# Long convolution by table transforms: even frequencies folded a second time, tables stored in two parts

## The reference

```python
def _hyena(hy, spec, skip):
    L = hy.shape[1]
    u = hy.astype(jnp.float32)
    z, g1, g2 = u[..., :D_HYENA], u[..., D_HYENA:2 * D_HYENA], u[..., 2 * D_HYENA:]
    for o, gate in enumerate((g1, g2)):
        conv = jnp.fft.irfft(jnp.fft.rfft(z, n=2 * L, axis=1) * spec[:, o], n=2 * L, axis=1)[:, :L]
        z = gate * (conv + z * skip[o].astype(jnp.float32))
    return z
```

## Time and profile before

| what | value |
|---|---|
| median of 3 runs | 3564.7 us (3564.47 to 3573.62) |
| the profiled execution, its own time | 3566.57 us |
| its span in the profile | 3564.8 us |
| mean granted TensorE clock | 0.971 of 2.4 GHz |
| PE busy | 3332.7 us, 93% of the span |
| `phase_convolve`, PE's first to last matmul | 433.46 to 721.8 us |

### The profile page before, as it was taken

How to read it: one execution, slowest core, us unless ns; L and a number is a source line. 1 busy time by engine, 2 the same in 40 slices (tenths; PEclk the granted TensorE clock), 3 DMA queues, 4 the chain that set the end, 5 groups by cost and what they waited for, 6 DMA issues and landing times. The chain is left out here.

```text
span 3564.8 us, 40485 instructions
## 1 busy us (share of the span) xinstructions
PE 3332.7 (93%) x15544; PEld 2663.5 (75%) x15544; DVE 1758.4 (49%) x2739; ACT 1112.2 (31%) x2015; POOL 560.6 (16%) x378
## 2 busy tenths in 40 slices
PE   7999899976898899999999998988999899999998
PEld 5777688865786678888888776775567688888886
DVE  4415655565422446555544539789654332332434
ACT  4323344354322222111111433136674221211112
POOL 0002466722000001000001200000263200010010
PEclk9999999987999999999999999999999999999999
DMA  3232324412121113333321301123333121111111
GB/s 115 87 104 70 130 88 136 142 61 92 54 71 59 42 59 95 100 102 105 104 83 62 105 18 42 48 57 90 76 73 113 30 71 48 47 47 47 51 43 59
DMA packets 223644, 269.80 MB, mean 76 GB/s; under 512 B 17277, under 2 KB 150294, under 8 KB 221062
## 3 DMA queue, kind: packets, MB, share of 16 engines
q1 hardware_dynamic: 223496, 267.78, 24.4%
HBM read 219.16 MB, written 29.18 MB: 70 GB/s over the span
## 5 line engine op out<-in xcount | busy, mean ns | idle before, releaser
L193 PE MATMUL psum<-rounded,rounded 128*128 128x512 f32 (+2 forms) x3936 | 1537.7, 391 | 64.6 <-DVE rounded L222 51.6
L194 PE MATMUL psum<-rounded,rounded 128*128 128x512 f32 (+2 forms) x3936 | 1528.7, 388 | 0.0
L195 PE MATMUL psum<-rounded,rounded 128*128 128x512 f32 (+2 forms) x3936 | 1528.2, 388 | 0.0
L193 PEld LDWEIGHTS psum<-rounded,rounded 128*128 128x128 f32 x3936 | 746.6, 190 | 239.1 <-DVE rounded L222 56.8
L195 PEld LDWEIGHTS psum<-rounded,rounded 128*128 128x128 f32 x3936 | 746.1, 190 | 151.8
L194 PEld LDWEIGHTS psum<-rounded,rounded 128*128 128x128 f32 x3936 | 747.2, 190 | 148.9 <-issue 0.2
L3002 DVE TENSOR_TENSOR plain<-psum,plain 128x512 f32<-128x512 f32 x432 | 288.6, 688 | 110.4 <-PE psum L195 108.8
L3013 DVE TENSOR_TENSOR plain<-psum,plain 128x512 f32<-128x512 f32 x44 | 30.4, 692 | 425.1 <-ACT plain L2917 425.1
L3579 POOL TENSOR_TENSOR plain<-plain,plain 128x128 f32<-128x128 f32 (+3 forms) x64 | 97.3, 1530 | 563.4 <-ACT plain L3680 506.4
L3376 DVE TENSOR_SCALAR_CACHE_REDUCE plain<-plain,plain 128x384 bf16<-128x384 f32 (+2 forms) x204 | 181.8, 942 | 1.4
L2994 DVE TENSOR_TENSOR rounded<-plain,rounded 128x512 fp32r<-128x512 f32 x108 | 96.9, 897 | 166.0 <-ACT rounded L2906 165.9
(11 more groups left out here) (326 smaller groups left out, 3457.5 us busy)
## 6 DMA issues: line engine op xcount, KB each, us to landing
plain<-in_ff_w_dram SPq DMA_DIRECT2D x64, 512.0 KB, 5.4
plain<-in_w_ada_dram SPq DMA_DIRECT2D x96, 256.0 KB, 3.5
plain<-in_w_gu_dram SPq DMA_DIRECT2D x44, 512.0 KB, 5.0
plain<-in_w_in_dram SPq DMA_DIRECT2D x36, 512.0 KB, 4.0
rounded<-rounded SPq DMA_DIRECT2D x72, 256.0 KB, 3.4
plain<-in_c_fwd_dram SPq DMA_DIRECT2D x64, 256.0 KB, 2.6
plain<-in_w_down_dram SPq DMA_DIRECT2D x22, 512.0 KB, 3.7
fold<-plain SPq DMA_DIRECT2D x8, 1024.0 KB, 4.8
```

The lines of the kernel that those rows point to most:

```text
L193: nc.tensor.matmul(out, wh, xh, start=first, stop=False)
L194: nc.tensor.matmul(out, wh, xl, start=False, stop=False)
L195: return nc.tensor.matmul(out, wl, xh, start=False, stop=last)
```

## The change

A table is now stored in DRAM as two parts, high and rest, so a unit is 512 KB; ACT copies both with rounding in one instruction of 1024 columns, and POOL no longer takes part. Rows are put in another order: even rows, odd rows and their mirror images (`TOKENS`, `COLUMNS`), so that sums and differences of quarters can be formed. With them the signal's and the inverse's even frequencies need transforms over 256 rows instead of 512, and the odd ones share sums. The single rows that fall out of the symmetry (lags 0, 256, 512, 768) are stored by small DMAs and mended on one partition.

```diff
-FOLD_KB, HY_KB, HR_KB, HS_KB, ZFOLD_KB, DFT_RING_KB, MATS_KB, NYQ_KB = 6, 70, 118, 134, 150, 182, 198, 200.75
+FOLD_KB, HY_KB, HR_KB, HS_KB, ZFOLD_KB, DFT_RING_KB, MATS_KB, NYQ_KB, QUARTER_KB = 6, 70, 118, 134, 150, 182, 198, 201.5, 203.5
+SIGNAL_ORDER = (0, 1, 2, 3, 4, 6, 5, 7)
+SIGNAL_AT, INVERSE_AT, ROUND_UNITS = 16, 28, 36
...
-        self.core.nc.scalar.activation(self.ring[u % 4].hi, self.ring[u % 4].raw, ACT.Copy).then_inc(S["ft_hi"].sem, 1)
-
-    def low(self, pool, u):
...
+        self.core.nc.scalar.activation(self.ring[u % 4], self.raws[u % 4], ACT.Copy).then_inc(self.core.sig["ft_hi"].sem, 1)
...
+    for n, j in enumerate(SIGNAL_ORDER):
+        one, two = ps[:, (2 * n) % 8, :], ps[:, (2 * n + 1) % 8, :]
+        if n < 4:
+            pe.wait_ge(R.sem("act_free"), R.at("act_free", n + 5))
+        else:
+            pe.wait_ge(R.sem("dve_done"), R.at("dve_done", 2 * (n - 3)))
+        if j < 4:
+            cos, sin = ((0, 1), (6, 7)) if j < 2 else ((2, 3), (4, 5))
+            tables.products(pe, one, B + n, zfold, cos, True, j >= 2)
...
+            ins = tables.products(pe, two, B + n, zfold, sin, True, j != 0, block=2)
...
+        else:
+            u = B + 2 * n - 4
+            tables.products(pe, one, u, zfold, range(4, 8), True, True).then_inc(done, 1)
+            tables.products(pe, two, u + 1, zfold, range(0, 4), True, False)
+            mm3(nc, two, eighth[0:1, 0, :], eighth[0:1, 1, :], quarter.hi[0:1, 0, :], quarter.lo[0:1, 0, :], False, True).then_inc(done, 1)
...
+            tables.products(pe, one, B + n, y, (src, src + 1), True, False)
+            ins = tables.products(pe, two, B + n, y, (src + 2, src + 3), True, False, block=2)
...
+    pe.wait_ge(R.sem("y_lo"), R.at("y_lo", 8))
...
                 for n in range(4):
                     if R.o == 0:
                         load_folds(core, sp, folds[1], raws[1], 1, (n,))
                     else:
                         load_kept(core, sp, kept, n)
-                    tables.load_units(sp, B + 2 * UNITS + 4 + 2 * n, units[0:B + 2 * UNITS + 6 + 2 * n])
+                    tables.load_units(sp, at, units[0:at + 1])
+                    at += 1
...
             def fold_high(R, n):
                 act.wait_ge(R.sem("fold%d" % n), R.at("fold%d" % n, 16))
+                if n >= 1:
+                    act.wait_ge(R.sem("fold_fixed"), R.at("fold_fixed", 1))
...
-                    if 1 <= j <= 4:
-                        for n in (2 * j - 2, 2 * j - 1):
-                            act.wait_ge(R.sem("v_hi"), R.at("v_hi", n + 1))
-                            nc.scalar.activation(zfold.hi[:, n, :], zfold.raw[:, n, :], ACT.Copy).then_inc(R.sem("z_hi"), 1)
+                    if 1 <= j <= 2:
+                        act.wait_ge(R.sem("v_hi"), R.at("v_hi", j))
+                        nc.scalar.activation(zfold.hi[:, 4 * j - 4:4 * j, :], zfold.raw[:, 4 * j - 4:4 * j, :], ACT.Copy).then_inc(R.sem("z_hi"), 1)
...
+                for b in range(2):
+                    until(B + (signal_done(6) + 1, INVERSE_AT + 2)[b])
+                    for part, tiles in enumerate((slice(4 + b, TT, 2), slice(TT + b, TT + 4, 2))):
+                        act.wait_ge(R.sem("paired"), R.at("paired", 2 * b + part + 1))
+                        nc.scalar.activation(y.hi[:, tiles, :], y.raw[:, tiles, :], ACT.Copy).then_inc(R.sem("w_hi"), 1)
...
+                if R.o == 0:
+                    fold_low(rounds[1], 0)
+                    terms_of(R, 0)
+                    fix_folds(rounds[1])
+                    fold_low(rounds[1], 1)
+                    terms_of(R, 1)
+                    fold_low(rounds[1], 2)
+                    fold_low(rounds[1], 3)
+                    outputs(R, 0)
+                    outputs(R, 1)
+                    dve.wait_ge(R.sem("tile_gated"), R.at("tile_gated", 4))
+                else:
+                    terms_of(R, 0)
+                    outputs(R, 0)
+                    terms_of(R, 1)
+                    group_sums(0)
+                    group_sums(1)
+                    outputs(R, 1)
+                    group_sums(2)
+                    group_sums(3)
```

More of the change, by code:

```diff
@@ L73, in constants, with split_table @@
+def split_table(blocks):
+    x = np.stack(blocks)
+    short = lambda v: np.ldexp(np.round(np.ldexp(np.frexp(v)[0], 11)), np.frexp(v)[1] - 11)
+    high = short(x)
+    return np.concatenate([high, x - high], 2).astype(np.float32)
+def constants():
+    fwd, sig, inv, order = transforms()
     p = np.arange(P)
@@ L657, in store, with stored @@
         sp.wait_ge(S["pair_folded"].sem, S["pair_folded"].at(f + 1))
[L658 removed]
+        to, first = self.folds[o].rearrange("p (q j) c -> p q j c", q=4)[:, :, j, :], 1 if j < 2 else 0
+        sp.dma_start(to[first:P], self.out[first:P]).then_inc(S["fold_stored"].sem, 16)
+        if j < 2:
+            for q, row in enumerate(((0, 0, 3, 2), (0, 2, 1, 3))[j]):
+                sp.dma_start(to[0:1, q, :], self.both[0:1, row, :]).then_inc(S["fold_stored"].sem, 16)
+    def stored(self, f):
+        return sum(80 if j < 2 else 16 for o, j in self.pairs[0:f])
     def hidden(self, pe, layer):
@@ L995, in products, with rounded @@
-    def products(self, pe, out, u, src, at, first, last):
+            sp.dma_start(self.raws[u % 4], units[u]).then_inc(self.loaded[u % 4], 16)
+    def rounded(self, act, u):
+        act.wait_ge(self.loaded[u % 4], 16 * (u // 4 + 1))
+        self.core.nc.scalar.activation(self.ring[u % 4], self.raws[u % 4], ACT.Copy).then_inc(self.core.sig["ft_hi"].sem, 1)
+    def products(self, pe, out, u, src, tiles, first, last, block=0):
         nc, S, w = self.core.nc, self.core.sig, self.ring[u % 4]
-        pe.wait_ge(S["ft_lo"].sem, S["ft_lo"].at(u + 1))
-        for k in range(4):
-            ins = mm3(nc, out, w.hi[:, k, :], w.lo[:, k, :], src.hi[:, at + k, :], src.lo[:, at + k, :], first and k == 0, last and k == 3)
+        pe.wait_ge(S["ft_hi"].sem, S["ft_hi"].at(u + 1))
+        for n, k in enumerate(tiles):
+            ins = mm3(nc, out, w[:, block + n, :], w[:, 4 + block + n, :], src.hi[:, k, :], src.lo[:, k, :], first and n == 0, last and n == len(tiles) - 1)
@@ new lines, in _ @@
+                for p in range(2):
+                    if R.o == 0 and p == 1:
+                        fold_high(rounds[1], 1)
+                    for part in range(2):
+                        u = INVERSE_AT + 5 + 2 * p + part
+                        until(B + u)
+                        act.wait_ge(R.sem("aux_done"), R.at("aux_done", u))
+                        if p == 0:
+                            nc.scalar.activation(rows[part], ps[0:1, 2 * part + 1, :], ACT.Copy)
+                        nc.scalar.activation(kept_sums[:, p, part, :], ps[:, 4 * p + 2 * part, :], ACT.Copy).then_inc(R.sem("act_done"), 1)
@@ L1231, in _ @@
+            for n in range(4):
+                square(n)
         @block.gpsimd
@@ new lines, in terms_of @@
+            def terms_of(R, p):
+                for part in range(2):
+                    dve.wait_ge(R.sem("act_done"), R.at("act_done", 2 * p + part + 1))
+                    own, other = kept_sums[:, p, part, :], ps[:, 4 * p + 2 * part + 1, :]
+                    nc.vector.tensor_tensor(terms[:, p, 2 * part, :], own, other, ALU.add)
+                    if part == 0:
+                        last = nc.vector.tensor_tensor(terms[:, p, 1, :], own, other, ALU.subtract)
+                    else:
+                        last = nc.vector.tensor_tensor(terms[:, p, 3, :], other, own, ALU.subtract)
+                last.then_inc(R.sem("dve_free"), 1)
```

611 lines of the change are left out of this document (350 added, 261 removed).

## The result

| what | before | after |
|---|---|---|
| median of the timed runs | 3567.59 us (3564.47 to 3573.62, 4 runs) | 3690.49 us (3686.85 to 3695.60, 4 runs) |
| span of the profiled execution | 3564.8 us | 3693.8 us |
| mean granted TensorE clock | 0.971 | 0.944 |

The account below looks back on a forecast made before the run. PE's matmul count at 0.2268 us each was taken to bound the convolution. -65.3 + 1.7 + 1.4 + 6 + 9 + 6 + 9.7 + 6 = -25.5 us, so a median of 3539 to 3540 us, range 3515 to 3556.

Parts of the forecast that it names:

- ahead of it: Before the convolution stage: transposes with step 2, extra short steps and larger first units add 1.7 us (0 to 4).
- Slower: Rival, chance 0.08: table units land too late in the ring; 13 us lost at 5.4 us landing, net +16 at 7.
- What it removes: Convolution, two rounds: 288 fewer matmuls at 0.2268 us each, -65.3 us if PE still never waits.
- first filter: First round's filter stage: PE waits some tenths three times behind ACT's roundings, +1.4 us (0 to 4).
- it doesn't do what it says: Rival: matmuls on one partition or with fewer blocks cost more; given nothing of its own.
- The first inverse: First round's inverse: PE waits for the split odd spectrum behind unit 32's load and ACT's rounding, +6 us (3 to 9).
- Between the rounds: Second round's filter: PE waits at the tenth unit for ACT, behind DVE's signal fold, +9 us (4 to 13).
- waits mostly hidden: Rival, chance 0.25: queue delay small and DVE quicker, so waits and clock cost 3 + 4 + 3 + 1; -41.5, 3523.
- The clock: PE runs at the lower clock after three long waits in the stage, 2 us each, +6 us (0 to 8).
- The end: After the last product, DVE's remaining outputs and sums end 16.1 us after PE instead of 6.4, +9.7 us (7 to 12).
- What would show it: Profile signs: 15256 matmuls, six PE waits in the stage, three short and three long, and a longer gap before group norm.
- The last sign: Forecast wrong if DVE reaches the folding of the signal sooner than 28 us after the last product.

Follow-up runs that it names:

- e1: The changed kernel with fold-block stores for j < 2 cut into partitions 1 to 112 and 113 to 127; 3541.66 us, ratio 0.9927.
- e3: As e1, but the store is cut into partitions 1 to 63 and 64 to 127; 3546.21 us in one run.
- e8: As e1, but the store is cut at partition 97, into 96 and 31 partitions; 3576.32 us.
- e2: The kernel before, with only the four fold-block stores for j < 2 cut into partitions 0 to 126 and partition 127; 3693.15 us, ratio 1.0354.
- e9: The changed kernel, 127-partition store kept, with the four one-partition stores issued ahead of it instead of behind; 3691.64 us.

## Why the prediction was wrong

- **The step that failed** is "ahead of it", which had +1.7 us. It priced transposes, short steps and the first units, and left out the stores of the fold blocks, though the change gives them 127 partitions, four small stores behind them and a wait of POOL. Measured, the stage starts 149.1 us later. 129.6 of it are the seven waits (132.3 against 2.7), 2.2 the two behind (8.1 and 4.3 against 6.8 and 3.5), and the rest, some 17, is PE at the lower of its two clocks (0.50 granted, 1.2 GHz) behind each long wait, four times: 3.78 us for four matmuls that take 1.98 otherwise, and then 8 to 11 distances of 0.43 instead of 0.23. With the store cut (e1) the stage starts 1.5 us later than before. The other terms of that step were right: eight transposes take 1.11 us with a step of 2, against 1.04.
- **No rival covered it.** "Slower" was the starved table ring. It didn't come: in e1 a unit of 512 KB lands in a median of 3.6 us in the filter and signal stages (forecast 3.7). In the inverse stages, where the 1 MB blocks stand between the units, the median is 6.3, above the 6.1 that would have lost the gain had every unit needed it, but only 16 of the 72 units are such. Behind ACT's table roundings PE waits 4.5 us in all. The ring stretch moves 183 GB/s (forecast about 190).
- **What it removes** holds: 288 matmuls at 0.2268 us, 972 in the stage instead of 1260. The trace has 15240 in all, not the 15256 forecast: the group norm needs no reversing matrix any more and has 32 records instead of 48, which the sum left out.
- **The stage's sum** was -36.9 us (-65.3 + 1.4 + 6 + 9 + 6 + 6). Measured -37.3, and -36.5 in e1. The number came out, the terms did not. Measured as distances between two starts less 0.2268, the waits behind the first take 10.8 us where 22.4 were given: none in the first filter (1.4 given), 2.6 and 2.5 at the two inverses (6 each), 1.0, 0.8 and 3.8 in the second filter (9). The switches between one partition and 128 take 9.7, which the rival "it doesn't do what it says" was given nothing for. That they nearly cancel is luck, though the two are not quite apart: a PE held up by its switches arrives later and waits less.
- **The chains behind the long waits** were read rightly, and sized within 2.3 us. The first inverse: with T the end of the signal stage (673.46 us in after), PE was forecast to need the split at T + 13.2 and to get it at T + 19.4; it stood there at T + 14.7 and went on at T + 17.1. The products ended at T + 2.6 (forecast 4), and the unit behind the fold blocks was ready at T + 12.6 (forecast 15). Between the rounds: ACT got the folded signal 31.4 us after the last product (forecast 32), and PE waited at the unit that was named, the tenth, but needed 30.6 us to get there and not 27.7, 1.9 of that in the two short waits. So the waits came out short by two things in about equal parts: tables and products that were ready a little earlier, as "waits mostly hidden" said of the queue, and a PE that arrived later than its count of matmuls says.
- **The clock** was given 6 and took 8.7 us against 2.4 before, 6.3 more. The forecast tied it to three waits of 6 to 9 us; it followed three of 2.5 to 3.8, with 7 to 13 matmuls at the lower clock behind each. How many is not fixed: e1 and e3 have the same stage, and in e3 the wait of 2.5 us at the first inverse has none behind it.
- **The end** was +9.7 and is +9.3, DVE busy 17.9 of 20 us there.
- **What lies behind the group norm** was given nothing, and took 7.9 us in after and 17.7 in e1's profile, for a reason that is open (above).
- **The sum, once the store is mended:** +1.5 - 36.5 + 9.3 = -25.7 us; forecast -25.5. With the 17.7 behind it that is -8.0, which is what e1's profiled execution gained (3558.48 against 3566.57). e1's median lies 24.7 us below its before; that this fits -25.5 rests on a rest of the program near 2833 us in the runs that were not profiled, which no trace shows.
- **What would show it:** the order of the waits in the second filter and at both inverses came as said, with ACT idle on `in_c_inv_dram` and on DVE's signal fold as named; the first filter's three short ones did not. The last sign was set wrong: DVE reaches the folding of the signal 23.6 us after the last product, sooner than 28, but the forecast's own sum (32 less 8.3) has it at 23.7. A second slip: 440 and the three steps behind it add up to 446.2, not 447.5; nothing rested on it.

## What to carry to other kernels

Read each DMA of a change for its partition count before its bytes: taking one partition off a 128-partition transfer made it last about 40 us instead of a median of 4.8, and cutting it into 112 and 15 costs one more issue and gave the time back. When listing what a change adds, go through the diff line by line and give every new transfer and every new wait on its completion its own price, also in stages that the change isn't about. Before calling a stage shorter by a few microseconds, see how much it differs among profiles that share it (248.3 to 251.8 us here), and count what the edit changes instead. And give a dozen saved microseconds in one stage no credit until a timed run shows them, when a later stage moves by as much.

## What the hardware did that was not expected

- A DMA over 127 or 31 partitions goes at 22 to 27 GB/s with 0.07 of the 16 DMA engines busy; 112, 96, 64, 63 and 15 show no such stretch (after, e1, e3, e8).
- While it runs, SP's queue is held at the next transfer, even a small one: a 2 KB store for 33.9 us (after), an 8 KB store for 33.6 (e2), a 512 KB load issued 7 us later for 27 (e9); behind 31 partitions a 2 KB store for 5.4 (e8).
- PE pays 0.20 us for each switch between matmuls on 128 partitions and on one, in either direction, spread over two distances (9.7 us for 48 switches, 7.3 for 36); the matmuls in between are 0.23 us apart, nearly the usual pace.
